# NSA layers: gate products, first scores and value products between products of few columns, and the shifted positions in two parts

## What is computed

```
q, k_c, v_c, k_s, v_s, k_w, v_w, gates = split(h @ w_in)     # 16 heads in 4 groups of 4, head size 64
gates = sigmoid(gates)                                       # 3 per head
kc = gelu(blocks(k_c + pos_k) @ k_w1) @ k_w2                 # 15 compressed keys per group
vc = gelu(blocks(v_c + pos_v) @ v_w1) @ v_w2
p_cmp = masked_softmax(q @ kc);   o_cmp = p_cmp @ vc
o_slc, o_win = causal attention over (k_s, v_s) and over (k_w, v_w)
out = (gates[0] * o_cmp + gates[1] * o_slc + gates[2] * o_win) @ w_out
```

## Time and profile before

| | us |
|---|---|
| median of 3 runs | 2254.62 (2253.14 to 2255.53) |
| the profiled execution, its own time | 2255.41 |
| its span from first to last instruction | 2253.4 |
| PE busy | 2204.2 (98%) |
| DVE busy | 1784.0 (79%) |
| ACT busy | 1165.1 (52%) |
| mean granted TensorE clock | 0.994 |

### The profile page before, as it was taken

The page is one execution under the profiler, slowest core; times in us unless marked ns, Lnnn a source line. Parts: engine busy times, 40 slices in busy tenths (PEclk is TensorE's granted clock), DMA queues, the critical chain, the costliest instruction groups (busy, mean ns, idle before and its releaser), DMA issues.

```text
span 2253.4 us, 37874 instructions
## 1 busy us (share of the span) xinstructions
PE 2204.2 (98%) x15228; PEld 1970.2 (87%) x15228; DVE 1784.0 (79%) x3504; ACT 1165.1 (52%) x2044; POOL 0.2 (0%) x4
## 2 busy tenths in 40 slices
PE   7999999999999999999999999999999999999998
PEld 7878889898889988896988887898888889979998
DVE  7788978689887898878898766577877876478888
ACT  4685556565544655458655634544222136376443
POOL 0000000000000000000000000000000000000000
PEclk9999999999999999999999999999999999999999
DMA  7416665466665566650666532024554523334563
GB/s 244 141 60 224 234 203 197 156 211 234 198 211 183 207 237 199 213 195 21 217 237 203 174 120 79 1 76 152 175 171 157 167 91 106 132 94 160 205 224 123
DMA packets 70158, 373.57 MB, mean 166 GB/s; under 512 B 7392, under 2 KB 16736, under 8 KB 37984
## 3 DMA queue, kind: packets, MB, share of 16 engines
q1 hardware_dynamic: 61472, 361.52, 46.9%
q10 hardware_dynamic: 8512, 9.63, 1.4%
HBM read 369.03 MB, written 1.05 MB: 164 GB/s over the span
## 4 chain that ended last, share of the span: by engine, by line
PE 84%; DVE 9%; ACT 3%; DMA 3%; issue 1%; ACTq 0%; DVEq 0%
PE ps L494 81%; DVE w_lo L2009 3%; DMA w_raw<-weights 2%; DVE hid_f L2392 1%; DVE hid_f L2414 1%; PE ps L838 1%; PE ps L775 1%; ACT w_hi L1345 1%; PE ps L822 1%; ACT hid_f L1545 0%; DVE ps L2043 0%; DVE v_sb L2522 0%; DVE a_both L2009 0%; DVE X L2135 0%; DVE X L2282 0%
## 5 line engine op out<-in xcount | busy, mean ns | idle before, releaser
L494 PE MATMUL ps<-a_both,w_hi 128*128 128x256 f32 (+1 forms) x4864 | 1057.8, 328 | 18.0 <-DVE a_both L2066 10.6
L494 PEld LDWEIGHTS ps<-a_both,w_hi 128*128 128x128 f32 x4864 | 808.4, 190 | 92.8 <-issue 15.4
L2009 DVE TENSOR_TENSOR w_lo<-w_raw,w_hi 128x1024 fp32r<-128x1024 f32 (+1 forms) x632 | 708.1, 1148 | 94.3 <-ACT w_hi L1345 85.8
L494 PE MATMUL ps<-a_both,w_lo 128*128 128x256 f32 (+1 forms) x3136 | 714.6, 292 | 0.0
L1345 ACT CAST w_hi<-w_raw 128x1024 fp32r<-128x1024 f32 (+2 forms) x446 | 412.7, 974 | 353.5 <-DMA w_raw<-weights 352.2
L494 PEld LDWEIGHTS ps<-a_both,w_lo 128*128 128x128 f32 x3136 | 521.4, 191 | 24.0
L494 PE MATMUL ps<-hid_both,w_hi 128*128 128x512 f32 (+2 forms) x2216 | 528.9, 348 | 5.1 <-DVE qk L3040 1.3
L494 PEld LDWEIGHTS ps<-hid_both,w_hi 128*128 128x128 f32 x2216 | 381.9, 189 | 59.2 <-issue 9.7
L494 PE MATMUL ps<-hid_both,w_lo 128*128 128x256 f32 (+2 forms) x1460 | 340.4, 305 | 0.0
L494 PEld LDWEIGHTS ps<-hid_both,w_lo 128*128 128x128 f32 x1460 | 236.4, 190 | 17.0
L1351 ACT CAST w_hi<-w_raw 128x1024 fp32r<-128x1024 f32 (+2 forms) x186 | 190.1, 1022 | 3.2 <-DMA w_raw<-weights 2.7
(11 more groups left out here) (236 smaller groups left out, 1907.7 us busy)
## 6 DMA issues: line engine op xcount, KB each, us to landing
w_raw<-weights SPq DMA_DIRECT2D x250, 1024.0 KB, 4.8
pe_sb<-weights SPq DMA_DIRECT2D x96, 512.0 KB, 5.6
w_raw<-weights SPq DMA_DIRECT2D x64, 704.0 KB, 4.0
pe_sb<-na_bias ACTq DMA_DIRECT2D x32, 128.0 KB, 2.3
X<-x_t SPq DMA_DIRECT2D x2, 512.0 KB, 7.0
X<-c_rows ACTq DMA_DIRECT2D x2, 512.0 KB, 4.1
qk<-qk ACTq DMA_DIRECT2D x4, 256.0 KB, 7.2
qk<-ctx_t ACTq DMA_DIRECT2D x1, 1024.0 KB, 5.4
```

What stands on the lines that cost most here:

```text
L494: return nc.tensor.matmul(out, stationary, moving, start=start, stop=stop)
L2009: return v.tensor_tensor(out, a, b.bitcast(F32), ALU.subtract)
```

## The change

On TensorE the gate products are made in three pieces, four groups ahead of the compressed keys, two behind them and two in the middle of the compressed values. The scores of item 0 move from behind the compressed scores to ahead of them, and the compressed scores are made in two halves of 8 products with half of `value_half(0)` between them. The two transposes of `gates_t` move from ahead of the scores to behind the second half of the compressed scores. The first result of the unit is now the compressed key and the second the gates, and ScalarE copies them in that order; `gates_copied` is replaced by the count `taken["A"]`. On VectorE the low part of the gelu results for keys comes ahead of the casts for values. The shifted positions of the values are added in two calls of four instructions, with the first half of the next `w_lo` between them, and `blocks_low(1)` stands ahead of a `skip` (which makes one unit's `w_lo`) in place of behind it. SyncE's order is the same. The diff, cut to its core:

```diff
-            def pair_attention(name, src, beside):
+            def pair_attention(name, src, beside, begun=0):
...
-                    if i < N:
+                    if begun <= i < N:
...
-                u, [(gb, gp, (g_ready, _)), (kb, kp, (k_ready, _)), (vb, vp, (v_ready, _))] = start_unit("AAD")
+                u, [(kb, kp, (k_ready, _)), (gb, gp, (g_ready, _)), (vb, vp, (v_ready, _))] = start_unit("AAD")
+                c0 = 2 * P + 2 * HD
                 start_product("A", gp)
...
+                def gates(ks):
+                    for k in ks:
+                        xh, xl = a[k]
+                        c = slice(c0 + k * 3 * HEADS, c0 + (k + 1) * 3 * HEADS)
+                        weights_at(c)
+                        out = ps[0:3 * HEADS, gb, 0:S]
+                        mm(out, w_hi[:, u % SLOTS, c], xh, k == 0, False)
+                        mm(out, w_hi[:, u % SLOTS, c], xl, False, False)
+                        last = mm(out, w_lo[:, u % SLOTS, c], xh, False, k == KD - 1)
+                    return last
+
+                def compressed_values(groups):
+                    for g in groups:
+                        last = tm(ps[:, vb, g * HD:(g + 1) * HD], u % SLOTS, lambda m: slice(2 * P + m * HD, 2 * P + (m + 1) * HD),
+                                  [(vg_hi[:, (m * GROUPS + g) * P:(m * GROUPS + g + 1) * P],
+                                    vg_lo[:, (m * GROUPS + g) * P:(m * GROUPS + g + 1) * P]) for m in range(2)])
+                    return last
+
+                def compressed_scores(b):
+                    for t in range(2 * REP):
+                        c = (b * 2 * REP + t) * 2 * CS
+                        last = mm(ps[:, CMP_BANK, c:c + 2 * CS], q_sb[:, t, b * P:(b + 1) * P], k_cmp[:, t // REP, :], True, True)
+                    return last
+
+                gates(range(0, 4))
+                pe.wait_ge(nsa[j]["gelu_ready"], 1)
                 start_product("A", kp)
                 fm(ps[:, kb, 0:WIDE], u % SLOTS, 0, [(wide(kg_hi, m), wide(kg_lo, m)) for m in range(2)]
                    ).then_inc(k_ready, 1)
+                gates((4, 5))
+                pe.wait_ge(nsa[j]["gelu_ready"], 2)
                 start_product("D", vp)
-                for g in range(GROUPS):
-                    last = tm(ps[:, vb, g * HD:(g + 1) * HD], u % SLOTS, lambda m: slice(2 * P + m * HD, 2 * P + (m + 1) * HD),
...
-                last.then_inc(v_ready, 1)
-                pe.wait_ge(nsa[j]["gates_copied"], j + 1)
+                compressed_values((0, 1))
+                gates((6, 7)).then_inc(g_ready, 1)
+                compressed_values((2, 3)).then_inc(v_ready, 1)
+                pe.wait_ge(taken["A"], gp + 1)
+                pair_scores(f"nsa{j}", 0, PAIR_S[0])
+                compressed_scores(0)
+                window = {}
+
+                def value_piece(tt, piece):
+                    if (tt, piece) == (0, 0):
+                        window["unit"], window["made"] = start_unit("DD")
+                    bank, p, (ready, _) = window["made"][tt]
+                    if piece == 0:
+                        start_product("D", p)
+                    many = KD // 2
...
+
+                value_piece(0, 0)
+                compressed_scores(1).then_inc(nsa[j]["cmp_scores"], 1)
                 for tt in range(2):
...
                 last.then_inc(nsa[j]["gates_t"], 1)
-                pe.wait_ge(taken["A"], kp + 1)
-                for b in range(2):
-                    for t in range(2 * REP):
...
-                        last = mm(ps[:, CMP_BANK, c:c + 2 * CS], q_sb[:, t, b * P:(b + 1) * P], k_cmp[:, t // REP, :], True, True)
-                last.then_inc(nsa[j]["cmp_scores"], 1)
-                window = {}
...
                 def beside(i):
                     if i == 0:
-                        value_half(0)
+                        value_piece(0, 1)
                         pe.wait_ge(nsa[j]["cmp_shifted"], j + 1)
                         pe.wait_ge(nsa[j]["gates"], j + 1)
...
-                        value_half(1)
+                        value_piece(1, 0)
+                        value_piece(1, 1)
...
-                pair_attention(f"nsa{j}", a, beside)
+                pair_attention(f"nsa{j}", a, beside, begun=1)
                 u, made = next_unit("AAD")
                 bank, p, (ready, count) = made[0]
                 wait(act, ready, count)
-                nc.scalar.copy(gates_t, ps[0:3 * HEADS, bank, 0:S]).then_inc(s["gates_copied"], 1)
-                bank, p, (ready, count) = made[1]
...
                 for e in range(2):
                     for pair in range(2):
                         g = 2 * pair + e
                         ins = nc.scalar.copy(k_cmp[half(e), pair, e * CS:(e + 1) * CS], ps[half(e), bank, g * CS:(g + 1) * CS])
-                ins.then_inc(taken["A"], 2)
+                ins.then_inc(taken["A"], 1)
+                bank, p, (ready, count) = made[1]
+                wait(act, ready, count)
+                nc.scalar.copy(gates_t, ps[0:3 * HEADS, bank, 0:S]).then_inc(taken["A"], 1)
                 act.wait_ge(s["gates_t"], j + 1)
...
-                def add_positions(kv, shifted):
-
-                    for par in range(2):
+                def add_positions(kv, shifted, pars=(0, 1)):
+
+                    for par in pars:
...
-                    ins.then_inc(s["blocks"], 1)
+                    if pars[-1] == 1:
+                        ins.then_inc(s["blocks"], 1)
...
                 unit_around(queries(1), lambda u: moved_positions(0))
                 blocks_low(0)
-                unit_around(queries(2), lambda u: moved_positions(1))
+                u, made = next_unit("AA")
+                scaled(made[0], queries(2)(0))
+                add_positions(1, True, (0,))
+                split_half(u + 2, 0)
+                add_positions(1, True, (1,))
+                scaled(made[1], queries(2)(1))
+                split_half(u + 2, 1)
                 skip("")
                 ahead(scaled_unit(queries(3)))
                 step(v.memset(vg_hi.bitcast(F32), 0.0))
+                blocks_low(1)
                 skip("")
-                blocks_low(1)
                 ahead(keys(0))
...
                 step(v.tensor_copy(kg_hi, k_gel))
+                sync()
+                minus(kg_lo, k_gel, kg_hi).then_inc(s["gelu_ready"], 1)
...
                 for m in range(2):
                     step(v.tensor_copy(v_rep[0][:, m, :, :, 0:CS], rep[m]))
                 sync()
-                minus(kg_lo, k_gel, kg_hi).then_inc(s["gelu_ready"], 1)
                 for m in range(2):
```

More of the change, by code:

```diff
@@ L228, in program @@
                for n in ("nsa0", "nsa1", "moba0", "mla0", "na0")}
-        nsa_once = {e: sem(e) for e in ("gelu_t", "gates_copied", "gates_t", "gates", "cmp_scores", "cmp_shifted", "cmp_exp", "cmp_p", "cmp_t")}
+        nsa_once = {e: sem(e) for e in ("gelu_t", "gates_t", "gates", "cmp_scores", "cmp_shifted", "cmp_exp", "cmp_p", "cmp_t")}
         nsa = [{e: sem(f"{e}{j}") for e in ("shifted", "blocks", "blocks_hi", "blocks_ready", "gelu", "gelu_ready", "cmp_t_taken")} | nsa_once
@@ L946, in run_nsa @@
                    ).then_inc(k_ready, 1)
+                gates((4, 5))
+                pe.wait_ge(nsa[j]["gelu_ready"], 2)
                 start_product("D", vp)
-                for g in range(GROUPS):
-                    last = tm(ps[:, vb, g * HD:(g + 1) * HD], u % SLOTS, lambda m: slice(2 * P + m * HD, 2 * P + (m + 1) * HD),
-                              [(vg_hi[:, (m * GROUPS + g) * P:(m * GROUPS + g + 1) * P],
-                                vg_lo[:, (m * GROUPS + g) * P:(m * GROUPS + g + 1) * P]) for m in range(2)])
-                last.then_inc(v_ready, 1)
-                pe.wait_ge(nsa[j]["gates_copied"], j + 1)
+                compressed_values((0, 1))
[12 more added lines that the diff above has]
+                    many = KD // 2
+                    for k in range(many * piece, many * (piece + 1)):
+                        xh, xl = raw_tokens(tt)[k]
+                        c = slice(k * KV, (k + 1) * KV)
+                        weights_at(c)
+                        out, at = ps[:, bank, 0:KV], window["unit"] % SLOTS
+                        mm(out, xh, w_hi[:, at, c], k == 0, False)
+                        mm(out, xl, w_hi[:, at, c], False, False)
+                        last = mm(out, xh, w_lo[:, at, c], False, k == KD - 1)
+                    if piece == 1:
+                        last.then_inc(ready, 1)
+                value_piece(0, 0)
+                compressed_scores(1).then_inc(nsa[j]["cmp_scores"], 1)
                 for tt in range(2):
@@ L957, in run_nsa @@
                 last.then_inc(nsa[j]["gates_t"], 1)
-                pe.wait_ge(taken["A"], kp + 1)
-                for b in range(2):
-                    for t in range(2 * REP):
-                        c = (b * 2 * REP + t) * 2 * CS
```

(8 more changed lines are left out.)

10 lines of the change are left out of this document (removed).

## The result

The change made the kernel slower: 2262.93 us, median of 6 runs (2261.28 to 2266.53), against 2253.97 (2252.86 to 2257.61) in 6 runs before. The ratio is 1.0038 with a 95% interval of 1.0027 to 1.0048. That is 9.0 us more. The profiled execution took 2262.35 us with a span of 2260.3; the one before took 2255.41 with 2253.4.

A forecast was written before the change was run, and what follows sets the result against it. TensorE, busy 98% of the span, was taken as the bound, leaving gaps and clock to move the time. Late transposes 10.1, upstream waits -3.5 and clock 2.2 made 8.8 us on 2254.6: 2263.4 us, range 2257.5 to 2268.

The forecast's parts named there:

- the late transposes: Both NSA layers: late gate transposes delay the transposes of the compressed probabilities to 23.8 us behind the first gate product; costs 10.1 us.
- the clock behind the wait: TensorE after its new 6.4 us wait: the clock falls to half rate, costing 1.1 us per layer, 2.2 in all.
- the upstream waits: TensorE's two waits on `w_lo` and two on `blocks_low(1)`, ahead of the slow stretch: all four go, winning 3.5 us.
- T: Start of the gate transposes on TensorE; claimed to move from 6.19 to 12.3 us behind the first gate product.
- All of this follows T: VectorE's chain to `cmp_shifted` and `cmp_p` hangs on the gate transposes' start, 8.17 and 11.41 us behind it, not on compressed scores.
- The step through the casts: ScalarE's first output unit casts stand behind the sigmoid, which waits for the gate transposes; VectorE's `w_lo` pair waits for these casts.
- What the clock can win: Compressed scores to transposes of compressed probabilities, both layers: a clock that stayed up would be worth 7.9 us.
- Rival A: Clock stays at 2.4 GHz and TensorE's waits upstream go: 11.4 us faster, 2243.2 us; chance 0.07.
- Rival B: The attention behind partly absorbs the delay and the clock returns at once: 5.3 us given back, 2258 us; chance 0.15.
- Rival C: Clock falls earlier, ahead of the gate transposes: 1.5 + 1.8 us lost in one or both layers, 2266.7 or 2270; chance 0.18.

The follow-up runs named there:

- e1_turns_early: The changed kernel with the two gate transposes put back ahead of item 0's scores; 2251.64 us, ratio to before 0.9988.
- e8_turns_late: The kernel before with only the two gate transposes moved behind the compressed scores; 2266.41 us, ratio to before 1.0047.
- e4_casts_first: The changed kernel with ScalarE's casts of the first output unit ahead of its wait for the gate transposes; 2255.01 us, ratio to before 1.0005.
- e3_filled: The changed kernel with 52 and 18 unread products ahead of the waits for `cmp_shifted` and `cmp_p`; 2263.59 us, ratio to before 1.0038.
- e6_item1_first: `e5_pieces` with VectorE's item 1 maxima ahead of the compressed sums and ScalarE's item 1 exponentials ahead of its copies; 2247.43 us, ratio to before 0.9968.
- e2_upstream_alone: The kernel before with only the shifted positions added in two calls and `blocks_low(1)` moved; 2250.37 us, ratio to before 0.9975.
- e7_mix_alone: `e1_turns_early` without the upstream part: positions in one call, `blocks_low(1)` where it was; 2255.65 us, ratio to before 1.0007.
- e5_pieces: `e1_turns_early` with the second 128 tokens' window values made in two pieces ahead of the two waits; 2250.90 us, ratio to before 0.9984.

## Why the prediction was right, point by point

The forecast was 2263.4 us and the median is 2262.93, 9.0 above before where the sum said 8.8. In the two profiles, up to the last item of the second NSA layer, the terms are 9.6 us for the late transposes (said 10.1), 2.7 for the clock behind the wait (2.2) and -3.5 for the upstream waits (-3.5), 8.8 together. The mechanism is right. That the total agrees to half a microsecond is in part luck: the runs of one kernel lie up to 5 us apart, and a stretch with the same instructions differs by about 1 us between profiles.

- *The gate transposes come late: 10.1 us.* Right. T was said to be 12.3 us behind the first gate product and is 12.13 in both layers; the wait 6.4 us, measured 6.29 and 6.30; the turns 23.8 us behind, measured 23.60. The cost to the turns is 5.66 + 3.97 = 9.63 us. The offsets T + 0.74, 1.82, 8.17 and 11.41 came out to the hundredth, since nothing but T moved in that chain. "All of this follows T" held before the change in the first layer only: in the second, VectorE waited 1.52 us for the slow compressed scores and `cmp_shifted` came at T + 9.65. The sum is untouched, since it takes the turns before from the rows. `e1_turns_early` (11.3 us less than the change) and `e8_turns_late` (11.4 more than before) show the cause from both sides; these two include what the clock does behind it.
- *The step through the casts.* Right: `e4_casts_first` leaves TensorE's order as it is and takes 7.9 us off.
- *The clock behind the wait: 2.2 us.* Right in kind and near in size. To item 2 it is 2.07 and 1.57 us; the attention takes up 0.45 and 0.47 of that, which leaves 2.7 us in all, inside the stated ends of 0 and 3.9 per layer. It is read from two profiles and not shown in the time: `e3_filled`, which should have won it back, did not. The granted clock went from 1.00 to 0.50 in the wait. The Trainium skill's rule, cited in the prediction, on long idle gaps between bursts of products ("TensorE: Matmul & The Clock Gate", section "Why this matters for your kernels") agrees here. It speaks of long gaps; in `e6_item1_first` the clock fell behind a single wait of 1.81 us as well.
- *The upstream waits: -3.5 us, all four go.* The size is right, one detail wrong. Three of four went; the first layer's wait for `w_lo` stayed, at 0.42 us, because VectorE's half there itself waited 1.58 us for ScalarE's cast. The two stretches that hold the waits are 1.13 and 2.39 us shorter after. By medians the part alone is worth 4.8 us (`e2_upstream_alone`, interval 3.4 to 7.7), and 4.0 between `e7_mix_alone` and `e1_turns_early`.
- *What the clock can win: at most 7.9 us.* It was a ceiling, and nothing here came near it. TensorE did run the narrow products at full speed, and `e7_mix_alone` shows that this alone is worth nothing that can be measured: TensorE then waits until G + 18.0 for `cmp_p`, where before the turns stood at G + 17.94 and G + 19.63.
- *Rival A* needed `cmp_shifted` by T + 1.8 and failed where said. Even with the transposes early the waits are 0.9 and 2.3 us: the prediction's condition for A was too weak, since `cmp_p` is a second wait.
- *Rival B* happened in small: the attention took up 0.9 us where B asked for 5.3.
- *Rival C* did not happen in the change's profiled execution, but did in those of `e3_filled` and `e4_casts_first`, whose products ahead of the transposes are the change's. T came 3.24 and 1.54 us later there, and 1.54 and 5.01, against a price of 3.3 per layer. So it is a matter of the execution. The change's longest run, 2266.53 us with a mean clock of 0.990 against 0.993 or 0.994 in the others, fits it; without a timeline of that run it is not shown.

## What to carry to other kernels

When a small operation is moved, follow what stands behind its consumer on the consumer's engine: here two transposes of 0.3 us, late in both layers, cost 11 us, because ScalarE's sigmoid waited for them, weight casts stood behind the sigmoid, and VectorE's masks behind the casts. A slow clock in a stretch is worth only what the next wait allows; look where the other engines' chain ends before counting its time as a gain. Covering such a wait with work that is due anyway won nothing clear by itself (`e5_pieces`, 0.7 us); together with an order of VectorE and ScalarE that makes first what TensorE asks for first, it won 4.2 us (`e6_item1_first` against `e1_turns_early`).

## What the runs showed of the hardware

- The granted clock fell with TensorE 100% busy, on the products of 32 columns or on the item's scores just ahead of them, and whether it does so varies between executions with the same instructions there. In the change's profile it stayed at 1.00 through them in both layers; in that of `e4_casts_first` it fell to 0.50 in both (these windows of it: busy all the time, clock 0.50), and in that of `e5_pieces` in the second layer only. In the kernel before the turns stand at G + 17.94 and G + 19.63, in `e2_upstream_alone`, with the same order from G on, at G + 19.63 and G + 18.01.

```profile
87.80:90.80 3.00, 3.00 (x15) 0.50 0.52 218
1010.00:1020.00 10.00, 10.00 (x48) 0.50 0.31 107
```

- It also fell behind a single wait of 1.81 us (`e6_item1_first`) and behind waits of 0.91 and 2.31 us close together (`e1_turns_early`), not only behind the change's wait of 6.3 us.
- In the first layer ScalarE's cast ahead of the wait for `w_lo` starts when a weight load has landed, and that varies with nothing edited there: from 42.67 us (`e8_turns_late`) to 45.35 (`e6_item1_first`). With the positions added in two calls, TensorE did not wait where the cast started by 44.01 us (`e1_turns_early`) and waited 0.42 us at 44.27 (the change) and 1.49 us at 45.35. So tenths of a microsecond there say nothing of an edit.
